# An encoder layer on one core: w_ada loaded as whole rows in two halves of channels behind x, x turned once and kept, rotary angles first, first q and k tiles in pairs

## The chip, the cores and the metric

One Trainium2 chip, of which the kernel uses one core. The time is device time in microseconds (us) of one execution; it is the median over several runs. TensorE is called PE (its weight loads PEld), VectorE DVE, ScalarE ACT, GpSimd POOL, SyncE SP. SP issues nearly all transfers.

## The reference

The layer has one sequence of 512 positions and 1,024 channels. What matters here is its beginning and what first uses it:

```python
mod = silu(c) @ w_ada + b_ada                  # w_ada: 1024 x 3072
shift, scale, gate = split(mod, 3)
h = rms_norm(x, norm_pre) * (1 + scale) + shift
proj = h @ w_in                                # w_in: 1024 x 11264
qa, ka, va, za, qd, kd, vd, zd, gm = split(proj, ...)
qa, ka = rope(qa, positions), rope(ka, positions)
# windowed attention with dilations 1, 4, 16 over qa, ka, va; differential
# attention over qd, kd, vd; gates, two projections, w_out, rms_norm
out = x + gate * rms_norm(y, norm_post)
```

Everything is float32. Before any product with w_in can be made, x's row norms and the first 2,048 columns of `silu(c) @ w_ada` are needed; the gate columns are needed only at the very end.

## The kernel before

**Split products.** A float32 product is made as three passes of rounded operands (`PASSES`): high by high, high by low, low by high. Each operand is cut into `_hi` (an ACT copy in the rounded type) and `_lo` (the difference, made by POOL or DVE).

**Weights.** w_in is cut into blocks of 256 columns, a block into two halves of 4 x 128 channels (k = 0 to 3 and 4 to 7). SP loads a half (512 KB) into one of three `raw` slots (`load_half`, L524), waiting until POOL has made the low part of the half three before. ACT makes the high part (`cut_hi`, L784), POOL the low one (`cut_lo`, L674). Halves 0 to 5 are those of blocks 0 (q), 1 (k) and 2 (v), in the order (0,0), (1,0), (0,1), (1,1), (2,0), (2,1); halves 6, 7 belong to block 3, the next q block.

**Order.** The work is laid out in ticks, and each engine runs through the same ticks in its own program. Tiles 0 to 3, the two q and two k tiles of 128 rows by 512 positions, are computed ahead of tick 8, all four at once, in four PSUM banks of `proj`: for each k the products of all four tiles (L1519 to L1525). Then come four v tiles (ticks 8 to 11), block 3 (ticks 12 to 15) with the first attention step's scores at tick 14, and so on, until PE's last tick.

**The modulation.** For each of the eight k, SP loads two column blocks of w_ada of 128 columns, scale and shift, all 1,024 rows of them (`load_ada`, rows of 512 bytes), into one of two buffers; DVE sums them over the eight row blocks weighted with silu(c) (`sum_ada`, eight instructions of 256 elements per partition); PE sums over the partitions with a matmul against ones (`modulation`, eight small products); three tiny DVE instructions make `ab`, the factor and the offset. PE turns x for that k (`x_turn`, four transposes into `score`), ACT makes `h_f` and `h_hi` from it, POOL `h_lo` (L689), and PE may make the products of that k. Column pair 0 is loaded between x tiles 1 and 2; the others stand in SP's queue among the weights. The buffers are freed by `ada_used`.

**The rotation.** ACT copies a finished q or k tile out of its bank (`rope_copy`, L817); SP's transfers swap the halves of the heads (four issues); DVE multiplies the swapped copy by the sine, POOL the other by the cosine (L704), DVE adds them into `rope_o`, ACT and DVE cut the sum into high and low. For tiles 0 to 3 the copies lie in `zd`, and one swap of four issues (L575) waits for all four copies (`rope_copied` 4). The angles themselves are computed by DVE (L1051 to L1061) after the last `ab`; ACT takes the sines after the four copies (L923, L925). Positions and the rotary constants are loaded by POOL's queue (L652, L653).

**Banks.** Tile 4 + i takes bank i again and waits for the copy of tile i, tile 8 takes the bank of the first v tile and waits until DVE has taken that tile's low part (`bank_free`, L1439). The first scores (`scores`, L1322) wait for the low parts of both q and both k tiles (`rope_lo_done`).

## Time and profile before

| | us |
|---|---|
| three runs: lowest, median, highest | 897.79, 899.67, 900.72 |
| profiled execution: span from first to last instruction (no other time is given with it) | 900.2 |
| PE busy in it | 820.2 (91%) |
| DVE, ACT, POOL busy | 461.5, 360.2, 499.6 |
| first product with w_in starts at | 34.6 |
| first score starts at | 102.5 |

The span is the profiled execution's first to last instruction on this one core. Busy times are sums over an engine's instructions; matmuls are pipelined, and their ends are modelled. "PEclk" or granted clock is the share of 2.4 GHz that was granted to PE: 1.00 is 2.4 GHz, 0.50 is 1.2 GHz. A row of waits says who waited for whom, the total, how often, and the longest.

### The profile page before, as it was taken

To read this page: it belongs to the slowest core of one execution; us is meant where nothing else is said; L and a number is where in the kernel's file an instruction comes from. 1 tells how busy PE (TensorE), PEld (TensorE's weight loads), DVE (VectorE), ACT (ScalarE), POOL (GpSimd) and SP (SyncE) were. 2 spreads that over 40 slices of the span, in tenths; PEclk is the share of its full clock that TensorE was granted. 3 is DMA by queue.
4 is the path that set the end of the run, shared out by engine and by line. 5 is a ranking of instruction groups with operands and counts; after the bars stand their busy time and mean duration, and the time that the engine had idled before them with its cause. 6 is when DMAs were issued, how large, how long until landed. Compare 5 with 4: busy or idle time off the path is not lost.

```text
span 900.2 us, 12651 instructions
## 1 busy us (share of the span) xinstructions
PE 820.2 (91%) x4622; PEld 687.3 (76%) x4622; DVE 461.5 (51%) x743; ACT 360.2 (40%) x774; POOL 499.6 (56%) x657
## 2 busy tenths in 40 slices
PE   1569799999999999999986889999999999999797
PEld 0458579888888888889765668887887778888697
DVE  2885587454444444325466767758756652112122
ACT  3333344344444444333443244545546442313210
POOL 2574555354564656347579665645646456648900
PEclk9999899999999999999999798999999999999899
DMA  9774282223333323223633222222221213324421
GB/s 248 196 213 109 83 277 85 90 76 97 104 107 106 106 84 106 93 95 95 169 110 93 83 67 75 71 82 84 71 71 48 71 48 116 94 71 141 140 90 52
DMA packets 92852, 94.87 MB, mean 105 GB/s; under 512 B 8269, under 2 KB 84086, under 8 KB 92662
## 3 DMA queue, kind: packets, MB, share of 16 engines
q1 hardware_dynamic: 92496, 93.64, 34.2%
q0 software_dynamic: 240, 0.39, 0.5%
q8 instruction: 37, 0.61, 0.3%
q14 instruction: 25, 0.20, 0.1%
q10 hardware_dynamic: 54, 0.02, 0.0%
HBM read 78.21 MB, written 5.34 MB: 93 GB/s over the span
## 4 chain that ended last, share of the span: by engine, by line
PE 60%; POOL 12%; DVE 9%; issue 7%; DMA 5%; ACT 4%; SPq 3%; DVEq 0%; POOLq 0%; ACTq 0%
PE proj L1482 41%; POOL w_lo L679 6%; PE score L1361 4%; PE proj L1565 4%; PE sums L1407 3%; DMA ada<-in_w_ada 3%; PE turned L1378 3%; PE sums L1409 2%; PE score L1336 2%; POOL rope_x L704 1%; DVE ada_sum L1014 1%; POOL h_lo L679 1%; DVE dstat L1128 1%; ACT junk L909 1%; DMA rope_s<-rope_x 1%
## 5 line engine op out<-in xcount | busy, mean ns | idle before, releaser
L679 POOL TENSOR_TENSOR w_lo<-raw,w_hi 128x256 fp32r<-128x256 f32 x408 | 328.2, 836 | 222.2 <-ACT w_hi L793 222.0
L1482 PE MATMUL proj<-h_hi,w_hi 128*128 128x512 f32 x608 | 253.5, 417 | 9.5 <-POOL h_lo L689 8.2
L1482 PE MATMUL proj<-h_hi,w_lo 128*128 128x512 f32 x608 | 241.7, 397 | 0.0
L1482 PE MATMUL proj<-h_lo,w_hi 128*128 128x512 f32 x608 | 240.7, 396 | 0.0
L1482 PEld LDWEIGHTS proj<-h_hi,w_hi 128*128 128x128 f32 x608 | 116.4, 191 | 45.8 <-issue 10.3
L1482 PEld LDWEIGHTS proj<-h_hi,w_lo 128*128 128x128 f32 x608 | 116.3, 191 | 26.5
L1482 PEld LDWEIGHTS proj<-h_lo,w_hi 128*128 128x128 f32 x608 | 116.9, 192 | 21.1
L793 ACT ACTIVATE w_hi<-raw 128x1024 fp32r<-128x1024 f32 x102 | 106.3, 1053 | 13.0 <-PE proj L1482 7.7
L704 POOL TENSOR_TENSOR rope_x<-rope_x,cos_t 128x512 f32<-128x512 f32 x36 | 55.1, 1531 | 86.7 <-DMA rope_s<-rope_x 86.7
L1151 DVE TENSOR_TENSOR at_lo<-turned,at_hi 128x512 fp32r<-128x512 f32 x64 | 44.0, 687 | 64.6 <-ACT at_hi L895 64.0
L877 ACT ACTIVATE probs<-score,dstat 128x512 f32<-128x512 f32 x64 | 43.4, 684 | 59.4 <-DVE dstat L1128 59.4
L1407 PE MATMUL sums<-v,at_hi 128*128 128x128 f32 (+1 forms) x256 | 61.2, 309 | 4.6 <-DVE at_lo L1151 4.6
L885 ACT ACTIVATE probs<-score,rows_out 128x128 f32<-128x128 f32 (+1 forms) x96 | 37.5, 400 | 67.2 <-DVE rows_out L1135 67.2
L1409 PE MATMUL sums<-v,at_lo 128*128 128x64 f32 (+1 forms) x256 | 57.7, 234 | 0.0
L895 ACT ACTIVATE at_hi<-turned 128x512 fp32r<-128x512 f32 x64 | 38.1, 595 | 45.0 <-PE turned L1378 44.5
L1378 PE MATMUL turned<-ident,probs 128*128 128x128 f32 x256 | 39.7, 278 | 17.0 <-DVE za L1226 13.9
L1407 PEld LDWEIGHTS sums<-v,at_hi 128*128 128x128 f32 x256 | 48.5, 190 | 7.9 <-DVE at_lo L1151 6.3
L1378 PEld LDWEIGHTS turned<-ident,probs 128*128 128x128 f32 x256 | 31.1, 142 | 26.8 <-DVE za L1226 15.0
L1409 PEld LDWEIGHTS sums<-v,at_lo 128*128 128x128 f32 x256 | 48.9, 191 | 2.0
L1482 PE MATMUL proj<-w_hi,h_hi 128*128 128x256 f32 x160 | 46.6, 291 | 0.0
L1482 PE MATMUL proj<-w_lo,h_hi 128*128 128x256 f32 x160 | 45.3, 283 | 0.0
L1482 PE MATMUL proj<-w_hi,h_lo 128*128 128x256 f32 x160 | 45.2, 283 | 0.0
(236 smaller groups left out, 1523.0 us busy)
## 6 DMA issues: line engine op xcount, KB each, us to landing
raw<-in_w_in SPq DMA_DIRECT2D x88, 512.0 KB, 3.6
rope_s<-rope_x SPq DMA_DIRECT2D x144, 64.0 KB, 2.3
ada<-in_w_ada SPq DMA_DIRECT2D x16, 512.0 KB, 6.2
zd<-in_w_ada SPq DMA_DIRECT2D x8, 512.0 KB, 5.1
raw<-in_w_proj_b SPq DMA_DIRECT2D x8, 512.0 KB, 3.4
raw<-in_w_out SPq DMA_DIRECT2D x8, 512.0 KB, 3.4
...
```

The lines of the kernel that those rows point to most:

```text
L679: ins = nc.gpsimd.tensor_tensor(lo[:, k, :], raw[:, n % RAW, k, :], hi.bitcast(F32)[:, k, :], ALU.subtract)
L704: nc.gpsimd.tensor_tensor(at, at, cos_t[:], ALU.mult).then_inc(rope_cos_done, 1)
L793: nc.scalar.activation(w_place(half)[0], raw[:, n % RAW, :, :], ACT.Copy).then_inc(w_hi_done, 1)
L877: ins = nc.scalar.activation(probs[:, s.s % 2, i, :], score[:, i, :], ACT.Exp, bias=dstat[:, s.s % 2, i:i + 1], accum_out=den0(s) if i == ...
L885: ins = nc.scalar.activation(probs[:, s.s % 2, 0, i * w:(i + 1) * w], score[:, s.s % 2, i * w:(i + 1) * w], ACT.Exp, bias=rows_out[:, qt, ...
L895: nc.scalar.activation(at_hi[:, s.s % 2, :], turned[:], ACT.Copy).then_inc(t_hi_done, 1)
L1151: tt_(at_lo[:, s.s % 2, :], turned[:], at_hi[:, s.s % 2, :].bitcast(F32), ALU.subtract).then_inc(t_read, 1)
L1361: ins = mm(bank[:, i * w + at:i * w + at + n_k], q[a][rows_, s.head // 2, qt * P:(qt + 1) * P], k[b][rows_, s.head // 2, key:key + n_k], s ...
L1378: ins = nc.tensor.transpose(turned[:, m * P:(m + 1) * P], probs[:, s.s % 2, 0, m * P:(m + 1) * P], ident[:])
L1407: mm(sums[:, to:to + 2 * width].rearrange("p (w e) -> p w e", w=2), hi[:, col:col + P], v[:, kt, :, col0:col0 + width], start=first, stop= ...
L1409: ins = mm(sums[:, to:to + width], lo[:, col:col + P], v[:, kt, 0, col0:col0 + width], start=False, stop=last, skip_group_check=True)
L1482: ins = mm(dst, left, right, start=k == 0 and n == 0, stop=k == nk - 1 and n == 2)
```

## The change

- `ada` holds all eight row blocks of half of the channels: SP loads, behind the four x tiles and raw halves 0 and 1, eight pieces of 512 KB for channels 0 to 511 (rows of 2 KB, scale and shift), then eight for channels 512 to 1,023, each into the place of the piece of the first half, once DVE has used it. Raw halves 2 and 3 stand behind all of them.
- DVE's sums take eight instructions of 1,024 elements per half; `modulation` and `modulate` run twice.
- All eight k of x are turned ahead of the modulation, into six PSUM banks, and ACT copies them to `xt`, which is `zd`'s memory; `h_f` and `h_hi` read `xt`.
- `h_lo` of k = 4 to 7 is made by DVE, of k = 0 to 3 by POOL. The masks are made ahead of the first `cut_lo`.
- PE makes k = 0 to 3 for all four tiles, with the second modulation ahead of k = 3, then k = 4 to 7 for tiles 0 and 1, then for tiles 2 and 3. The swap is made in two pairs, ahead of loads 7 and 8.
- The angles stand first in DVE's queue, ahead of x's mean; the sines follow the scaling of x on ACT. Positions and constants are loaded by ACT's queue.

```diff
         x_in = sb("x_in", [P, NT, D], on=begin)
-        ada = sb("ada", [P, 2, KT, 2, P], on=begin)
-        ada_sum = sb("ada_sum", [P, 2, 2, 2, P], on=begin)
-        h_f = sb("h_f", [P, 2, S], on=begin)
+        ada = sb("ada", [P, KT, 2, S], on=begin)
+        ada_sum = sb("ada_sum", [P, 2, 2, S], on=begin)
...
+        xt = zd
+        def turn_place(k):
+            return score[:, k % 6, :] if k % 6 < 2 else proj[:, k % 6 - 2, :]
...
-            def load_ada(k):
-                if k >= 2:
-                    sp.wait_ge(ada_used, 2 * (k - 1))
-                src = w_ada[0].rearrange("(a p) n -> p a n", p=P)
-                for i in range(2):
-                    sp.dma_start(ada[:, k % 2, :, i, :],
-                                 src[:, :, i * D + k * P:i * D + (k + 1) * P]).then_inc(ada_loaded[k % 2], 16)
+            ada_rows = w_ada[0].rearrange("(a p) (r n) -> p a r n", p=P, r=3)
+            def load_ada(half, kk):
+                if half:
+                    sp.wait_ge(ada_used, kk + 1)
+                sp.dma_start(ada[:, kk, :, :], ada_rows[:, kk, 0:2, half * S:(half + 1) * S]).then_inc(ada_loaded[kk], 16)
...
             for tt in range(NT):
-                if tt == 2:
-                    load_ada(0)
                 sp.dma_start(x_in[:, tt, :], x[0, tt * P:(tt + 1) * P, :]).then_inc(x_loaded[tt], 16)
             load_half(0)
             load_half(1)
-            load_ada(1)
-            load_ada(2)
+            for half in range(2):
+                for kk in range(KT):
+                    load_ada(half, kk)
             load_half(2)
-            load_ada(3)
             load_half(3)
-            for k in range(4, KT):
-                load_ada(k)
...
             for n in range(4, next_half):
+                if n in (7, 8):
+                    pair = n - 7
+                    sp.wait_ge(rope_copied, 2 * pair + 2)
+                    for i in range(4):
+                        j = i ^ 1
+                        sp.dma_start(zd[32 * i:32 * i + 32, 4 + 2 * pair:6 + 2 * pair, :],
+                                     zd[32 * j:32 * j + 32, 2 * pair:2 * pair + 2, :]).then_inc(first_swapped[pair], 16)
                 load_half(n)
...
+            masks()
             for half in prep_at(-1)[:2]:
                 cut_lo(half)
-            for k in range(KT):
+            for k in range(KT // 2):
                 pool.wait_ge(h_hi_done, k + 1)
                 nc.gpsimd.tensor_tensor(h_lo[:, k, :], h_f[:, k % 2, :], h_hi[:, k, :].bitcast(F32),
                                         ALU.subtract).then_inc(h_lo_done, 1)
-                if k in (1, 2, 4, 6):
-                    cut_lo(halves[2 + (1, 2, 4, 6).index(k)])
-                if k == 3:
-                    masks()
+            for half in prep_at(-1)[2:]:
+                cut_lo(half)
             for t in range(8, LAST_TICK + 1):
-                for half in prep_at(t) if t < 12 else []:
-                    cut_lo(half)
-                for tile in tiles[:4] if t == 8 else rope_at(t) if t >= 12 else []:
+                for tile in tiles[2 * (t - 8):2 * (t - 7)] if t < 10 else rope_at(t) if t >= 12 else []:
                     swapped_wait(pool, tile)
                     if rope_no[tile.u] == 0:
                         pool.wait_ge(act_sin, 2)
                     at = rope_place(tile)[0]
                     nc.gpsimd.tensor_tensor(at, at, cos_t[:], ALU.mult).then_inc(rope_cos_done, 1)
-                for half in prep_at(t) if t >= 12 else []:
+                for half in prep_at(t):
                     cut_lo(half)
...
+            act.dma_start(rope_c[:], rope_rows).then_inc(pos_loaded, 16)
+            act.dma_start(merged[:].bitcast(I32), positions[0].partition_broadcast(P)).then_inc(pos_loaded, 16)
...
+            act.wait_ge(angle_done, 1)
+            nc.scalar.activation(sin_t[:], rope_s, ACT.Sin).then_inc(act_sin, 1)
+            act.wait_ge(angle_done, 2)
+            nc.scalar.activation(cos_t[:], rope_o[:], ACT.Sin).then_inc(act_sin, 1)
             for half in prep_at(-1)[:2]:
                 cut_hi(half)
             for k in range(KT):
                 act.wait_ge(x_turned, k + 1)
-                act.wait_ge(ab_done, k + 1)
-                if k >= 2:
+                nc.scalar.activation(xt[:, k, :], turn_place(k), ACT.Copy).then_inc(xt_done, 1)
+            for k in range(KT):
+                act.wait_ge(ab_done, k // 4 + 1)
+                act.wait_ge(xt_done, k + 1)
+                if k >= 6:
+                    act.wait_ge(h_lo_late, k - 5)
+                elif k >= 2:
                     act.wait_ge(h_lo_done, k - 1)
-                nc.scalar.activation(h_f[:, k % 2, :], score[:, k % 2, :], ACT.Identity, bias=ab[:, 1, k:k + 1],
+                nc.scalar.activation(h_f[:, k % 2, :], xt[:, k, :], ACT.Identity, bias=ab[:, 1, k:k + 1],
                                      scale=ab[:, 0, k:k + 1]).then_inc(h_f_done, 1)
-                nc.scalar.activation(h_hi[:, k, :], score[:, k % 2, :], ACT.Identity, bias=ab[:, 1, k:k + 1],
+                nc.scalar.activation(h_hi[:, k, :], xt[:, k, :], ACT.Identity, bias=ab[:, 1, k:k + 1],
                                      scale=ab[:, 0, k:k + 1]).then_inc(h_hi_done, 1)
-                if k in (1, 2, 4, 6):
-                    cut_hi(halves[2 + (1, 2, 4, 6).index(k)])
+                if k >= 3:
+                    for half in prep_at(-1)[k - 1:k] if k < KT - 1 else []:
+                        cut_hi(half)
             act.wait_ge(lam_dots, 1)
             nc.scalar.activation(lam[:, 2:4], lam[:, 0:2], ACT.Exp).then_inc(act_lam, 1)
...
-            act.wait_ge(angle_done, 1)
-            nc.scalar.activation(sin_t[:], rope_s, ACT.Sin).then_inc(act_sin, 1)
-            act.wait_ge(angle_done, 2)
-            nc.scalar.activation(cos_t[:], rope_o[:], ACT.Sin).then_inc(act_sin, 1)
...
-            def sum_ada(k):
-                dve.wait_ge(ada_loaded[k % 2], 32 * (k // 2 + 1))
-                if k >= 2:
-                    dve.wait_ge(mod_done, k - 1)
...
-            sum_ada(0)
...
-            dve.wait_ge(cols_done, 2)
-            for k in range(KT):
-                if 0 < k < KT - 1:
-                    sum_ada(k + 1)
-                mod = (turned, sums)[k % 2]
...
+            def sum_ada(half, kk):
+                dve.wait_ge(ada_loaded[kk], 16 * (half + 1))
+                total = ada_sum[:, half]
+                if kk == 0:
+                    ins = ts_(total, ada[:, kk], silu_c[:, 1, 0:1], None, ALU.mult)
+                else:
+                    dve.wait_ge(ada_used, KT * half + kk)
+                    ins = stt(out=total, in0=ada[:, kk], scalar=silu_c[:, 1, kk:kk + 1], in1=total,
+                              op0=ALU.mult, op1=ALU.add)
+                ins.then_inc(ada_used, 1)
+            def modulate(half):
+                mod, ks = (turned, sums)[half], slice(4 * half, 4 * half + 4)
+                at = lambda first: cols[:, first + 4 * half:first + 4 * half + 4]
+                dve.wait_ge(mod_done, half + 1)
+                link(tt_(ab[:, 0, ks], mod[:, 0:4], at(16), ALU.add))
+                link(stt(out=ab[:, 0, ks], in0=ab[:, 0, ks], scalar=1.0, in1=at(32), op0=ALU.add, op1=ALU.mult))
+                tt_(ab[:, 1, ks], mod[:, 4:8], at(8), ALU.add).then_inc(ab_done, 1)
+            dve.wait_ge(pos_loaded, 32)
...
+            dve.wait_ge(act_x_sq, NT)
+            ts_(st[:, 4:8], st[:, 0:4], 1.0 / D, EPS, ALU.mult, ALU.add).then_inc(x_mean_done, 1)
+            dve.wait_ge(rows_turned, 2)
+            nc.vector.tensor_copy(cols[:, KT:41], sums[:, KT:41]).then_inc(cols_done, 1)
+            dve.wait_ge(pow_done, 1)
+            for tt in range(2):
+                ts_(x_in[:, tt, :], x_in[:, tt, :], st[:, 8 + tt:9 + tt], None, ALU.mult).then_inc(x_norm_done, 1)
+            dve.wait_ge(cols_done, 2)
+            for kk in range(KT):
+                sum_ada(0, kk)
+            modulate(0)
+            for kk in range(KT):
+                sum_ada(1, kk)
+            dve.wait_ge(small_loaded, 64)
...
+            modulate(1)
+            for k in range(KT // 2, KT):
+                dve.wait_ge(h_f_done, k + 1)
+                dve.wait_ge(h_hi_done, k + 1)
+                tt_(h_lo[:, k, :], h_f[:, k % 2, :], h_hi[:, k, :].bitcast(F32), ALU.subtract).then_inc(h_lo_late, 1)
...
-            def modulation(k):
-                if k >= 2:
-                    pe.wait_ge(ab_done, k - 1)
-                if k == 1:
-                    pe.wait_ge(cols_done, 2)
-                pe.wait_ge(ada_used, 2 * (k + 1))
+            def modulation(half):
+                pe.wait_ge(ada_used, KT * (half + 1))
                 for i, side in enumerate((1, 0)):
-                    for part in range(2):
-                        ins = mm((turned, sums)[k % 2][:, i:i + 1], ada_sum[:, k % 2, part, side, :], ones[:, 0:1],
-                                 start=part == 0, stop=part == 1)
+                    for k in range(4):
+                        ins = mm((turned, sums)[half][:, 4 * i + k:4 * i + k + 1], ada_sum[:, half, side, k * P:(k + 1) * P],
+                                 ones[:, 0:1], start=True, stop=True, skip_group_check=True)
                 ins.then_inc(mod_done, 1)
             def x_turn(k):
-                if k == 0:
-                    pe.wait_ge(x_norm_done, 2)
-                    pe.wait_ge(x_norm_act, 2)
-                if k >= 2:
-                    pe.wait_ge(h_hi_done, k - 1)
+                if k >= 6:
+                    pe.wait_ge(xt_done, k - 5)
                 for tt in range(NT):
-                    ins = nc.tensor.transpose(score[:, k % 2, tt * P:(tt + 1) * P], x_in[:, tt, k * P:(k + 1) * P], ident[:])
+                    ins = nc.tensor.transpose(turn_place(k)[:, tt * P:(tt + 1) * P], x_in[:, tt, k * P:(k + 1) * P], ident[:])
                 ins.then_inc(x_turned, 1)
+            pe.wait_ge(x_norm_done, 2)
+            pe.wait_ge(x_norm_act, 2)
+            for k in range(KT):
+                x_turn(k)
+            pe.wait_ge(cols_done, 2)
             modulation(0)
-            x_turn(0)
-            for k in range(KT):
-                if k + 1 < KT:
-                    modulation(k + 1)
-                    x_turn(k + 1)
+            pe.wait_ge(xt_done, KT)
+            for k in range(KT // 2):
+                if k == 3:
+                    modulation(1)
                 pe.wait_ge(h_lo_done, k + 1)
                 for tile in tiles[:4]:
                     products(tile, [k])
+            for pair in (tiles[0:2], tiles[2:4]):
+                for k in range(KT // 2, KT):
+                    pe.wait_ge(h_lo_late, k - 3)
+                    for tile in pair:
+                        products(tile, [k])
...
```

The cut parts of the DVE program are in the section on the kernel: the angles (L1052 to L1061) stay as they are and now stand between `modulate` and the mean of x, and the lambda dots (L1045 to L1049) stand behind the sums of the second half. The single swap of L572 to L575 is gone.

## Rows read from the trace of the kernel before

**Rows 1.** Busy time by stretch: us from:to, length, busy (x instructions), granted clock, DMA share, GB/s.

```profile
34.50:78.90 44.40, 35.73 (x173) 29.17 (x172) 33.01 (x77) 15.81 (x23) 25.87 (x35) 0.92 0.65 184
78.90:90.30 11.40, 11.40 (x96) 11.26 (x94) 6.15 (x12) 4.24 (x6) 6.69 (x7) 1.00 0.55 138
90.30:102.50 12.20, 6.10 (x25) 4.24 (x24) 10.62 (x16) 5.04 (x9) 5.67 (x6) 0.97 0.14 44
102.50:108.70 6.20, 6.17 (x19) 4.87 (x20) 0.69 (x1) 3.92 (x8) 5.53 (x8) 0.51 0.27 87
120.00:390.00 270.00, 270.00 (x1591) 229.84 (x1591) 134.95 (x173) 119.59 (x308) 141.97 (x149) 1.00 0.33 101
390.00:600.00 210.00, 190.12 (x1072) 155.97 (x1071) 127.91 (x207) 85.00 (x178) 135.14 (x176) 0.96 0.33 97
```

**Rows 2.** Waits of PE: 34.4 to 102.5 us, then 102.4 to 390.

```profile
PE proj L1482 <- POOL h_lo L689: 8.2, 4, 3.6
PE proj L1482 <- DVE v L1102: 1.1, 1, 1.1
...
PE score L1350 <- DVE k_lo L1095: 5.0, 1, 5.0
```

**Rows 3.** Busy time of PE's product line (L1482) alone, in two stretches of twelve products.

```profile
34.50:38.70 4.20, 4.07 (x12) 1.00 1.13 319
52.10:55.00 2.90, 2.84 (x12) 1.00 0.52 135
```

**Rows 4.** The chain that ended last, its start: from us, us, what.

```profile
54.93 6.30 DMA raw<-in_w_in
...
81.42 4.94 DMA zd<-zd
```

**Rows 5.** Timeline of the start, ACT, DVE and PE: start us, us, engine, line, what.

```profile
18.86 1.87 PE L1503 MATMUL turned<-ones,ada_sum 128*128 128x1 f32 x8 [13.92 <-DVE ada_sum L1014]
...
19.49 0.17 DVE L1024 TENSOR_SCALAR st<-st 128x4 f32<-128x4 f32 x1 [0.68 <-ACT gate_row L782]
...
20.81 2.19 ACT L797 ACTIVATE x_in<-x_in,st 128x1024 f32<-128x1024 f32 x2 [1.36 <-POOL st L684]
```

**Rows 6.** Transfers: packets and rates from 0 to 9 us, then from 9 to 13.

```profile
DMA packets 2106, 2.14 MB, mean 237 GB/s; under 512 B 118, under 2 KB 1792, under 8 KB 2106
...
DMA packets 441, 0.35 MB, mean 88 GB/s; under 512 B 58, under 2 KB 369, under 8 KB 441
...
q0 software_dynamic: 111, 0.14, 83.1%
```

**Rows 7.** DVE's angle chain, groups of instructions by line: busy us, mean ns.

```profile
L1060 DVE SCALAR_TENSOR_TENSOR rope_x<-rope_x 128x512 f32<-128x512 f32 x1 | 0.7, 683 | 0.0
...
L1058 DVE TENSOR_SCALAR rope_x<-rope_x 128x512 f32<-128x512 f32 x1 | 0.4, 427 | 0.0
```

**Rows 8.** Groups of ACT by line, 20 to 83 us, shapes kept apart, and one of POOL, 24 to 58.

```profile
L808 ACT ACTIVATE h_f<-score,ab 128x512 f32<-128x512 f32 x8 | 6.2, 774 | 28.9 <-DVE ab L1039 15.0 <-issue 13.9
L793 ACT ACTIVATE w_hi<-raw 128x1024 fp32r<-128x1024 f32 x5 | 5.1, 1046 | 0.0
...
L923 ACT ACT_TABLE_LOAD x1 | 1.3, 1283 | 0.0
...
L689 POOL TENSOR_TENSOR h_lo<-h_f,h_hi 128x512 fp32r<-128x512 f32 x5 | 7.0, 1402 | 9.7 <-ACT h_hi L810 9.7
```

**Rows 9.** Transfers from 34 to 42 us, then from 115 to 119.

```profile
DMA packets 4378, 2.47 MB, mean 309 GB/s; under 512 B 70, under 2 KB 4378, under 8 KB 4378
...
DMA packets 456, 1.67 MB, mean 418 GB/s; under 512 B 48, under 2 KB 48, under 8 KB 456
```

**Rows 10.** The gate's sums on DVE (L1256), 128x1024: shortest, median, longest ns.

```profile
L1256 DVE SCALAR_TENSOR_TENSOR gate_row<-zd,silu_c,gate_row x7: 1272/1758/2306, 117.1 to 146.1; 128x1024 f32<-128x1024 f32 x7
```

**Rows 11.** DVE's timeline, the rotation of tiles 2 and 3, first and last instruction.

```profile
96.97 0.68 DVE L1078 TENSOR_TENSOR zd<-zd,sin_t 128x512 f32<-128x512 f32 x1
...
101.78 0.69 DVE L1095 TENSOR_TENSOR k_lo<-rope_o,k_hi 128x512 fp32r<-128x512 f32 x1 [0.36 <-ACT k_hi L831]
```

54 lines of the change are left out of this document (11 added, 43 removed).

## The prediction

> **What bounds the kernel now.** I first read busy time by stretch. From 120 to 390 us PE is busy 270.00 of 270.00 us at full clock; in the 68 us from the first product (34.5) to the first score (102.5) it is busy 53.2 us (35.73 + 11.40 + 6.10) [rows 1]. So the start is where PE lacks work, and what follows runs at PE's pace. PE's waits put names on it: 8.2 us for h_lo, 1.1 us for a bank that DVE had not emptied, 5.0 us for k_lo [rows 2]. Between waits it is slow as well: a k of twelve products takes 2.84 us in a warm stretch, but the first k after the long pause took 4.07 [rows 3], and after the 5 us wait the granted clock is 0.51, that is 1.2 GHz, for 6 us [rows 1]. The chain of waits shows what is behind h_lo and k_lo: a weight half that SP had queued behind the w_ada columns takes 6.30 us to come, and the swap of the heads' halves 4.94 [rows 4]. So the start is a chain "w_ada columns, sum, modulation, h, products" run eight times, then a rotation that waits for all four tiles. A microsecond by which the first score comes earlier should be a microsecond off the end. One stretch speaks against that: from 390 to 600 PE is busy 190.12 of 210.00 [rows 1]. The weights it waits for there are cut behind waits on PE's own products (`cut_hi`), so I take those stalls to move with PE.
>
> **The new order, step by step** (times from the span's start).
>
> *x first.* Before, x's mean stood at 19.49 [rows 5]. In the first 9 us the transfers carried 2.14 MB; from 9 to 13 lies a hole of 88 GB/s, in which POOL's own queue takes 83% of the engines for 0.14 MB [rows 6]. The lambda rows stay on that queue, so I keep the hole. x and the positions are 2.36 MB: in at about 10, the last square at 12. But DVE now does the angles ahead of the mean. Positions (0.26 MB) are issued on ACT's queue at about 2.5, beside the first two x tiles (1.05 MB): 1.31 MB at some 300 GB/s (the 2.14 MB of rows 6 went in the seven us that transfers ran) are in at 7. Bounds: 5.6 at 418 GB/s [rows 9], and 13, the end of the hole. The chain is seven short instructions of 0.43 to 0.48 and five long ones of 0.68 us alone [rows 7]: 6.5 us, ending at 13.5. Mean at 13.7, 5.8 us sooner. From mean to scaling 1.3, scaling 2.19 on ACT [rows 5]: 17.2; DVE's share ends at 16.5.
>
> *ACT.* Table load 1.28, two sines 1.2, two weight halves 2.1, eight new copies of turned x out of PSUM at under 0.77 each (h_f is the nearest row), some 5.3 [rows 8]: 27.1. PE's 32 turns lie beside this. The copies end before the modulation does and so cost nothing; without that cover, 5.3.
>
> *First half of w_ada.* x, raw halves, positions and lambda rows are 3.55 MB; after the hole, at the 309 to 418 GB/s of rows 9, the last raw lands at about 16.2. Then 4.19 MB in 2 KB rows: 309 was reached with rows of 512 bytes and 1 KB, 418 with 4 KB [rows 9]; I take 360, so 11.7 us: 27.9. The second half, piece by piece behind the sums, is in at 39.5. DVE now takes 8 instructions of 1,024 elements for 32 of 256. One takes 1.27 alone, 1.76 in the median and 2.31 at worst beside POOL [rows 10], the first of a half 0.75 as the scaling of x does. POOL writes the masks and cuts halves 0 and 1 meanwhile: 0.75 + 3 x 1.6 + 4 x 2.0 = 13.6, from 16.5: 30.1. Bounds: 29.2 (27.9 + 1.27) and 33.4 (0.75 + 7 x 2.31). Modulation: eight small products 1.87 [rows 5], three tiny DVE instructions 0.6: 32.6. h_f and h_hi 1.5, h_lo 1.4 [rows 8]: first product at 35.5. Before: 34.6. **The start of the products is a loss of 0.9 us.**
>
> *k = 0 to 3.* h comes every 1.5 us from ACT and 1.4 from POOL, PE needs 2.8: no gap. The first k takes 4.0, two more 2.8 each [rows 3]: 45.1.
>
> *Second half.* DVE from 32.6: 0.75 + 7 x 1.8 (POOL has h_lo and half 2 to cut beside it) = 13.4: 46.0. Bounds: 41 (last piece at 39.5) and 49.5. The lambda dots, 1.1, and three tiny instructions: ab at 47.7; PE's part 0.95 is done meanwhile. PE waits 45.1 to 47, makes k = 3 by 49.8, and h_lo of k = 4 is there at 47.7 + 1.5 + 0.7 = 49.9. Now ACT sets the pace, with a weight half of 1.0 between two k: 2.5 us each, k = 7 at 57.4. A k of one pair is 1.4 us of work, so the pair ends at 58.8, and the second pair, with all its inputs there, takes 4 x 1.4: 64.4. Before: 78.9. **14.5 us**, of which the one start above is -0.9 and the seven gaps and slow k after it 15.4. The weights come in time: raw 2 lands at 41.5, its low part is ready by 46, raw 5 follows at 50 and is wanted at 55.
>
> Row and rule can be weighed here. Beside POOL the long DVE instruction grew by 0.49 and 1.04 us [rows 10]. The Trainium skill, SBUF — State Buffer, section Who interferes with whom, makes the port pair that the two engines share an exclusive lock: who comes second blocks until the other instruction is through. By it four sums against an h_lo would take 1.27 + 1.40 each and two against a part of w_lo 1.27 + 0.7, and the second half 0.75 + 4 x 2.67 + 1.27 + 2 x 1.97 = 16.6, an estimate: 3.2 us more than mine, total 880. Rows 10 agree that they block each other, not that it is each time in full.
>
> *v block and first score.* v 11.4 [rows 1]: 75.8. **Bank wait 1.2 gone:** tiles 0 and 1 are copied by 60, swapped by about 65 (4.94 [rows 4]), and their rotation lies under the v block, so DVE takes the first v tile at about 68, 8 us before its bank is wanted. Products of the next q tile 2 x 2.84 = 5.7 (6.0 before): **81.5 for the first score.** Is k_lo there? Tiles 2 and 3 are copied at 65.7, swapped at 71, POOL's cosine product at 73; tiles 2 and 3 took 5.5 us from 96.97 to 102.47 before [rows 11]: 79. Yes, by 2.5 us: **5.0 us gone.** The four more issues of SP cost it 2.4 us each pair with two raw slots full: nothing.
>
> *After the score.* The 6.2 us at a clock of 0.51 [rows 1] held 3.1 us of loss. Half 9 and the pieces of the gate columns behind it come forward less than PE does, so I credit 2.0.
>
> **Sum.** 14.5 + 1.2 + 0.3 + 5.0 = 21.0 to the score, and 2.0: 23.0 us. Span 900.2 - 23.0 = 877.2. The page gives that execution no other time; 900.2 lies between the median 899.67 and the highest 900.72. Forecast: **877**.
>
> **Removed work worth nothing.** 48 of 64 small modulation products leave PE where it waited; four h_lo leave POOL, which waited too. SP's blocked issues behind `ada_used` release no one earlier than rows 9's rates do.
>
> **Rivals.**
> - *The rotation still ends last* (0.14). The last of the four swap issues was out at 81.4 [rows 4], 21.1 us ahead of the score. It would now be out 1.9 after the copies at 65.7; the same distance gives 88.7, 7.2 later: 884. For it: DVE takes v tiles between rotations, POOL's cosine products stand before half 6. Against: two of four tiles are under the v block.
> - *DVE bounds the start* (0.17). All long sums at 2.31 [rows 10]: 33.4 + 2.5 + 16.9 = 52.8 for 46.0: 6.8 later, 884. Positions at 13 instead of 7 give 6 us: 883. It shows as PE idle before k = 3.
> - *DVE hardly meets POOL* (0.08). Sums bound by transfers: k = 4 up to 5 us sooner, 869 to 872.
> - *The early time is given back* (0.04): 390 to 600 is paced by something not tied to PE. Time 900.
> - *Slower* (0.03). The angles stand at the head of DVE's queue; x's mean, the scaling and all sums are queued behind the positions' landing. Each microsecond after 7 is one lost (6 of them up to the end of the hole). From 33 us on the kernel is slower: 23.0 eaten and 2.7 more, 903. For it only the hole of rows 6.
> - *As forecast* (0.54): 873 to 882.
>
> **Range.** 869 to 887: below, the free DVE; above, the 884 of two rivals and 3 us for a clock that falls in the pair phase, where PE works 1.4 of each 2.5 us. Runs lie within 0.3% of each other, so 2.7 us can be told. Faster 0.54 + 0.14 + 0.17 + 0.08 = 0.93; same 0.04; slower 0.03.
>
> **What will show it.** x's mean at 14; eight sums ending near 30 and 46; first product within 2 us of 35.5; second pair without a gap from 59 to 64; first score at 81.5, no wait before it, clock 1.00 after it; PE 270 of 270 in the long stretch. Wrong would be: positions landing late, long sums at 2.3, a score that waits for k_lo, or PE idle later that was not there before.

## The result, and the profile of the changed kernel

The changed kernel took **892.92 us** (median of 4 runs, 892.13 to 893.5), the kernel before, run beside it, 900.19. The ratio is 0.9917 with a 95% interval of 0.9900 to 0.9934. So it is faster by some 7 us, a third of the 23 that were forecast, and 892.92 lies above the range of 869 to 887. The sign was right, the size was not.

The span of the profiled execution is 891.3 us; that of before is 900.2, the forecast for it 877.2. The miss to be explained is 14.1 us. First the stretches (columns: busy time and count for PE, PEld, DVE, ACT and POOL, then PE's granted clock, the DMA share and GB/s), which answer to [rows 1]:

```profile
20.00:40.80 20.80, 9.93 (x49) 9.70 (x50) 15.63 (x16) 13.47 (x20) 17.71 (x23) 0.77 1.03 372
40.80:54.00 13.20, 12.64 (x54) 10.23 (x55) 12.08 (x13) 3.85 (x5) 12.13 (x7) 0.84 0.03 10
54.00:70.40 16.40, 13.97 (x58) 10.23 (x57) 6.04 (x11) 11.28 (x15) 9.73 (x12) 1.00 0.36 98
70.40:89.00 18.60, 17.66 (x124) 16.25 (x123) 16.72 (x18) 7.75 (x13) 13.66 (x12) 1.00 0.48 140
102.00:106.40 4.40, 0.42 (x2) 0.00 (x0) 3.98 (x6) 2.75 (x7) 0.46 (x1) 1.00 1.01 359
106.40:115.00 8.60, 8.58 (x33) 7.12 (x34) 7.35 (x9) 4.29 (x12) 5.83 (x5) 0.60 0.99 326
```

The products of the first four tiles now end at 70.9 (78.7 before, each read from the start of the v block), and the v block with the next q tile keeps PE busy 17.66 of 18.60 us. But a hole stands where none was forecast: from 102.0 to 106.4 PE works 0.42 us, and then it goes at 1.2 GHz, half its upper level (mean granted clock 0.60 up to 115.0). PE's waits from 0 to 130 us, which answer to [rows 2], give it a name (us in total, times, longest):

```profile
PE turned L1505 <- DVE ada_sum L1017: 4.3, 1, 4.3
PE turned L1384 <- DVE at_lo L1157: 4.0, 1, 4.0
PE proj L1488 <- issue: 3.9, 1, 3.9
...
PE proj L1488 <- DVE h_lo L1067: 2.3, 3, 1.2
...
PE score L1356 <- DVE k_lo L1101: 0.9, 1, 0.9
PE sums L1505 <- DVE ada_sum L1017: 0.6, 1, 0.6
```

The waits for h_lo shrank from 8.2 to 2.3 and that for k_lo from 5.0 to 0.9, as the prediction had it. New is the one for `at_lo`, 4.0 us. Now the start itself, DVE's timeline, to be read beside [rows 5]:

```profile
12.36 0.43 DVE L1031 CAST rope_x<-merged 128x512 f32<-128x512 int32 x1 [7.48 <-DMA merged<-in_positions]
...
19.09 0.16 DVE L1043 TENSOR_SCALAR st<-st 128x4 f32<-128x4 f32 x1
...
21.91 0.88 DVE L1014 TENSOR_SCALAR ada_sum<-ada,silu_c 128x1024 f32<-128x1024 f32 x1
22.91 10.18 DVE L1017 SCALAR_TENSOR_TENSOR ada_sum<-ada,silu_c,ada_sum 128x1024 f32<-128x1024 f32 x7
36.82 0.16 DVE L1026 TENSOR_TENSOR ab<-turned,cols 128x4 f32<-128x4 f32 x1 [3.73 <-PE turned L1505]
...
37.29 0.74 DVE L1014 TENSOR_SCALAR ada_sum<-ada,silu_c 128x1024 f32<-128x1024 f32 x1
38.14 13.53 DVE L1017 SCALAR_TENSOR_TENSOR ada_sum<-ada,silu_c,ada_sum 128x1024 f32<-128x1024 f32 x7
...
53.71 0.16 DVE L1026 TENSOR_TENSOR ab<-sums,cols 128x4 f32<-128x4 f32 x1 [0.50 <-PE sums L1505]
```

DVE stands 7.48 us until the positions are there, at 12.36, and the mean of x follows the angles at 19.09, though the last square on ACT was done at 13.9. That is nearly where it stood before (19.49). The sums themselves went well: the first half took 11.2 us (13.6 forecast), the second 14.4 (13.4 forecast). PE's timeline for the same time:

```profile
33.24 3.54 PE L1505 MATMUL turned<-ones,ada_sum 128*128 128x1 f32 x16 [4.26 <-DVE ada_sum L1017]
40.65 0.77 PE L1488 MATMUL proj<-h_hi,w_hi 128*128 128x512 f32 x1 [3.87 <-issue]
41.21 0.63 PE L1488 MATMUL proj<-h_lo,w_hi 128*128 128x512 f32 x1
```

The modulation is 16 records, not 8, and takes 3.54 us; the first product starts at 40.65, 5.1 later than forecast and 6.0 later than before. At the other end of the start, DVE's four rotations (k_lo of tile 3 is what the first score waits for):

```profile
70.60 1.83 DVE L1084 TENSOR_TENSOR zd<-zd,sin_t 128x512 f32<-128x512 f32 x1 [4.33 <-DMA zd<-zd]
72.46 2.27 DVE L1094 TENSOR_TENSOR rope_o<-zd 128x448 f32<-128x448 f32 x2
...
76.53 1.22 DVE L1084 TENSOR_TENSOR zd<-zd,sin_t 128x512 f32<-128x512 f32 x1
...
82.42 1.22 DVE L1084 TENSOR_TENSOR zd<-zd,sin_t 128x512 f32<-128x512 f32 x1
...
86.10 0.69 DVE L1084 TENSOR_TENSOR zd<-zd,sin_t 128x512 f32<-128x512 f32 x1
...
88.22 0.69 DVE L1101 TENSOR_TENSOR k_lo<-rope_o,k_hi 128x512 fp32r<-128x512 f32 x1 [0.36 <-ACT k_hi L841]
```

The first score starts at 88.97 (102.5 before): 13.5 us sooner. The span is shorter by 8.9. What eats the rest lies in the 18 us behind it, here on ACT, POOL, SP's queue, DVE and PE in turn. (The second turns are PE's second group of turned attention probabilities, at 106.42; the third follow at 114.94.)

```profile
88.09 1.99 ACT L794 ACTIVATE w_hi<-raw 128x1024 fp32r<-128x1024 f32 x2
89.21 5.58 POOL L682 TENSOR_TENSOR w_lo<-raw,w_hi 128x256 fp32r<-128x256 f32 x8 [4.96 <-ACT w_hi L794]
92.04 3.14 SPq L536 DMA_DIRECT2D raw<-in_w_in  x2
95.23 2.41 SPq L558 DMA_DIRECT2D rope_s<-rope_x  x4
97.68 2.84 SPq L597 DMA_DIRECT2D zd<-in_w_ada  x4
102.15 0.86 DVE L1259 TENSOR_SCALAR gate_row<-zd,silu_c 128x1024 f32<-128x1024 f32 x1 [10.85 <-DMA zd<-in_w_ada]
102.93 0.68 DVE L1141 TENSOR_REDUCE rows_out<-score 128x2 f32<-128x512 f32 x1
105.67 0.69 DVE L1157 TENSOR_TENSOR at_lo<-turned,at_hi 128x512 fp32r<-128x512 f32 x1 [0.27 <-ACT at_hi L905]
106.42 1.08 PE L1384 MATMUL turned<-ident,probs 128*128 128x128 f32 x4 [4.00 <-DVE at_lo L1157]
114.94 0.60 PE L1384 MATMUL turned<-ident,probs 128*128 128x128 f32 x4
```

ACT cuts halves 8 and 9 only behind its last k_hi, so their low parts on POOL begin at 89.21. SP, which issues in order, can load into those slots from 92.04 on, and issues the swap of the next tile and then the gate columns behind that. DVE has the first gate instruction ahead of the row maxima of the second score, and stands for it 10.85 us. PE's next turns need the at_lo behind it. In the kernel before, the same two places, of the waits of PE and of the timelines of PE and DVE:

```profile
PE turned L1378 <- DVE at_lo L1151: 0.7, 1, 0.7
...
119.44 0.66 PE L1378 MATMUL turned<-ident,probs 128*128 128x128 f32 x4 [0.71 <-DVE at_lo L1151]
124.87 0.60 PE L1378 MATMUL turned<-ident,probs 128*128 128x128 f32 x4
...
115.28 0.75 DVE L1253 TENSOR_SCALAR gate_row<-zd,silu_c 128x1024 f32<-128x1024 f32 x1 [9.19 <-DMA zd<-in_w_ada]
```

The gate instruction comes 13.1 us sooner than there (102.15 for 115.28), nearly the whole 13.5. But PE got over its work between score and turns faster, as forecast: its clock is 1.00 there, where [rows 1] had 0.51 for 6 us. The same work, from the first score to the last product ahead of the second turns, took 15.8 us before (102.53 to 118.34) and 13.1 now (88.97 to 102.03), 2.8 less. That went into the wait, which grew by 3.3, from 0.7 to 4.0. Behind the wait PE goes at 1.2 GHz for 6.8 us, and from the second to the third turns it takes 8.5 us where it took 5.4 (106.42 to 114.94, 119.44 to 124.87): 3.1 more. From the third turns to the mark that the ledger below uses, both kernels take 88.9 us. So 3.3 + 3.1 - 2.8 = 3.6 us is the whole loss between score and mark.

**The ledger of the miss**, each line the measured time less the forecast one:

| point | forecast | measured | late | new here |
|---|---|---|---|---|
| first product | 35.5 | 40.65 | 5.1 | 5.1 |
| second pair's end | 64.4 | 70.9 | 6.5 | 1.4 |
| first score | 81.5 | 88.97 | 7.5 | 1.0 |
| span | 877.2 | 891.3 | 14.1 | 6.6 |

The 6.6 behind the score split at a mark that every kernel here has: the first product of the middle scores with `mask_near`, at 213.8 before and 203.8 now, in a stretch in which PE waits for nothing. From score to mark it was 111.3 us and is 114.9, a loss of 3.6 where a credit of 2.0 had been given; and from the mark to the end 686.4 and 687.5, a loss of 1.1 (5.6 and 1.1 make the 6.6 to rounding). So the start is worth **10.0 us** at the mark. Below, each kernel is measured there too, since what follows the mark varies by some us between executions (680.6 to 687.9 us over the kernels here, whose instructions behind it are the same). PE's mean granted clock behind the mark is 0.99 in the shortest, e12, and 0.98 in all others, so the clock has a part in it; how large, no run shows.

### The profile page after: what moved, and what is told of

The parts are those of the page before. It is cut to its first block, busy times and chain, and to the rows that moved or that the text cites. A ratio compares the mean times of both kernels' runs of the same rounds, so it can differ in the third digit from the quotient of the medians.

```text
span 891.3 us, 12543 instructions
## 1 busy us (share of the span) xinstructions
PE 818.0 (92%) x4590; PEld 685.6 (77%) x4590; DVE 455.3 (51%) x681; ACT 364.9 (41%) x782; POOL 504.2 (57%) x651
## 4 chain that ended last, share of the span: by engine, by line
PE 62%; POOL 12%; DVE 10%; issue 7%; ACT 5%; DMA 3%; SPq 1%; ACTq 0%; DVEq 0%; POOLq 0%
PE proj L1488 43%; POOL w_lo L682 6%; PE score L1367 4%; PE proj L1573 4%; PE sums L1413 3%; PE turned L1384 3%; DVE ada_sum L1017 3%; PE score L1342 2%; PE sums L1415 2%; POOL h_lo L682 1%; POOL rope_x L703 1%; DVE dstat L1134 1%; ACT junk L919 1%; DMA merged<-in_positions 1%; ACT probs L887 1%
## 5 line engine op out<-in xcount | busy, mean ns | idle before, releaser
L682 POOL TENSOR_TENSOR w_lo<-raw,w_hi 128x256 fp32r<-128x256 f32 x408 | 332.9, 847 | 216.6 <-ACT w_hi L794 216.4
```

What stands on the lines that cost most here:

```text
L682: ins = nc.gpsimd.tensor_tensor(lo[:, k, :], raw[:, n % RAW, k, :], hi.bitcast(F32)[:, k, :], ALU.subtract)
```

## The experiments

All are edits of the changed kernel unless another is named, each timed beside the kernel before, whose median was 898.2 to 901.0 in the different sets; so medians are compared by their ratios. "Mark" is the start of the first `mask_near` product. Scores, turns and marks come from one trace of each kernel. What one trace can tell is seen on e6: its instructions are those of the kernel before up to the score, and yet score and mark come 1.3 and 1.4 us sooner. So a mark that differs by up to some 1.4 us (e1, e3, e5, e7, e10, e12, e13) says little by itself.

| run | median | ratio (95%) | first score | second turns | third turns | mark | wait for at_lo |
|---|---|---|---|---|---|---|---|
| kernel before | 900.19 | | 102.5 | 119.4 | 124.9 | 213.8 | 0.7 |
| changed kernel | 892.92 | 0.9917 (0.9900 to 0.9934) | 89.0 | 106.4 | 114.9 | 203.8 | 4.0 |
| e1 lambda rows late | 891.06 | 0.9884 (0.9852 to 0.9917) | 86.8 | 104.4 | 114.0 | 202.9 | 4.1 |
| e2 angles late | 888.97 | 0.9871 (0.9842 to 0.9899) | 89.1 | 105.7 | 111.1 | 201.0 | 0.4 |
| e3 gate sums late | 889.57 | 0.9883 (0.9851 to 0.9915) | 88.8 | 102.2 | 107.6 | 202.8 | 1.7, at 115 |
| e5 no pairs | 891.34 | 0.9917 (0.9891 to 0.9943) | 90.3 | 107.1 | 112.5 | 202.4 | 0.8 |
| e6 gate sums late, before | 900.36 | 1.0001 (0.9980 to 1.0022) | 101.3 | 117.1 | 122.4 | 212.4 | none |
| e7 two sums ahead | 893.76 | 0.9947 (0.9923 to 0.9971) | 89.4 | 106.7 | 115.2 | 204.1 | 2.3 |
| e8 positions first | 888.44 | 0.9883 (0.9853 to 0.9914) | 85.1 | 102.7 | 112.2 | 201.1 | 4.2 |
| e9 halves 8, 9 sooner | 888.98 | 0.9895 (0.9871 to 0.9920) | 90.5 | 107.0 | 112.3 | 201.3 | none |
| e10 PE kept busy | 887.09 | 0.9853 (0.9825 to 0.9881) | 89.7 | 106.7 | 115.2 | 204.1 | 2.0 |
| e11 = e8 + e9 | 884.48 | 0.9827 (0.9798 to 0.9856) | 86.7 | 103.2 | 108.5 | 197.5 | none |
| e12 = e11 + e10 | 883.75 | 0.9824 (0.9795 to 0.9854) | 88.0 | 104.2 | 109.6 | 198.5 | none |
| e13 = e11 + e3 | 885.29 | 0.9832 (0.9804 to 0.9859) | 86.8 | 101.7 | 107.0 | 196.9 | none |

### What holds x's mean at 19.1

**e1**, the lambda rows (POOL's own queue) issued behind the power instead of ahead of the masks:

```
-            for i, v in enumerate((lambda_q1, lambda_k1, lambda_q2, lambda_k2)):
-                pool.dma_start(lam_in[:, i, :], ...).then_inc(small_loaded, 16)
...
             nc.gpsimd.tensor_tensor(st[:, 8:12], st[:, 4:8], half_c[:, 0:4], ALU.pow).then_inc(pow_done, 1)
+            for i, v in enumerate((lambda_q1, lambda_k1, lambda_q2, lambda_k2)):
+                pool.dma_start(lam_in[:, i, :], ...).then_inc(small_loaded, 16)
```

> The changed kernel with the four lambda rows issued by GpSimd after the power and not at the start. Theory A (the software queue's rows hold everything behind them from 9 to 11 us, the positions too): positions land at about 9 instead of 12.3, the last x tile by 11, x's mean at about 16 instead of 19.1, and the end comes 2 to 3 us sooner. Theory B (positions stand behind the x tiles on the same sixteen engines): the hole goes, positions still land at 11 to 12.5, less than 1 us at the end.

The positions landed at 10.0 instead of 12.31, the last square came at 11.5 and the mean at 16.73; the first score came 2.2 us sooner, the mark 1.0.

**e8**, in addition the positions and the rotary rows issued first on ACT's queue, ahead of the small rows:

```
+            act.dma_start(rope_c[:], rope_rows).then_inc(pos_loaded, 16)
+            act.dma_start(merged[:].bitcast(I32), positions[0].partition_broadcast(P)).then_inc(pos_loaded, 16)
             act.dma_start(rows[8:32, :], b_ada.rearrange("a (r p) -> (a r) p", p=P)).then_inc(rows_loaded, 16)
...
-            act.dma_start(rope_c[:], rope_rows).then_inc(pos_loaded, 16)
-            act.dma_start(merged[:].bitcast(I32), positions[0].partition_broadcast(P)).then_inc(pos_loaded, 16)
```

> The changed kernel with the positions and rotary constants issued first on ScalarE's queue and the lambda rows after the power. Theory A (positions at the head of VectorE's queue are what delays the mean): positions land at 5 to 6, angles end at 12, mean at 12.5 instead of 19.1; the sums are then bound by transfers, first score about 5 us sooner, end 4 to 6 us sooner. Theory B (issue order on another queue does not matter, all sixteen engines serve x first): positions at 9 to 10 as with the late lambda rows alone, mean at 16.7.

DVE's timeline of this kernel:

```profile
7.08 0.43 DVE L1031 CAST rope_x<-merged 128x512 f32<-128x512 int32 x1 [2.08 <-DMA merged<-in_positions]
...
13.82 0.16 DVE L1043 TENSOR_SCALAR st<-st 128x4 f32<-128x4 f32 x1
...
16.59 0.73 DVE L1014 TENSOR_SCALAR ada_sum<-ada,silu_c 128x1024 f32<-128x1024 f32 x1
17.45 5.46 DVE L1017 SCALAR_TENSOR_TENSOR ada_sum<-ada,silu_c,ada_sum 128x1024 f32<-128x1024 f32 x4
24.59 4.64 DVE L1017 SCALAR_TENSOR_TENSOR ada_sum<-ada,silu_c,ada_sum 128x1024 f32<-128x1024 f32 x3 [1.68 <-DMA ada<-in_w_ada]
```

This is the timeline that the prediction had: positions at 7, mean at 13.8 (13.7 forecast), sums from 16.6 to 29.2. The first score came at 85.1, 3.9 us sooner, and the second turns 3.7, behind a wait of 4.2 us for at_lo. The mark came only 2.7 us sooner, because the stretch at 1.2 GHz behind that wait lasts 10.2 us here, where it lasted 6.8: from the second to the third turns PE takes 9.5 us for 8.5. The sums now wait 1.68 us for a piece: the transfers have become what bounds them.

**e2**, the angle chain moved behind DVE's last h_lo and the two sines behind the copies of the first four tiles; the positions land when they will:

```
-            dve.wait_ge(pos_loaded, 32)
-            link(nc.vector.tensor_copy(rope_x, merged[:].bitcast(I32)))
-            ... (the angle chain)
             dve.wait_ge(act_x_sq, NT)
...
                 tt_(h_lo[:, k, :], ..., ALU.subtract).then_inc(h_lo_late, 1)
+            (the angle chain)
```

> The changed kernel with the rotary angles back behind the last h_lo on VectorE and the sines behind the four rope copies. Theory A (positions and angles at the head of VectorE's queue delay the mean of x, and that delay goes through to the end): mean at 14.1 instead of 19.1, sums of the first half from 17, first score about 5 us sooner (84), end 4 to 5 us sooner. Theory B (the time to the score is not what sets the end: what follows waits for the gate columns anyway): first score sooner, end within 1 us. Theory C (the angles are then late themselves): score waits for k_lo, no gain or a loss of some us.

The mean stood at 14.66 with nothing ahead of it but the squares. The score came no sooner (PE waited 3.7 us for k_lo, because the angles now delay the rotations), yet the mark came 2.8 us sooner. That is the clock and not the angles: behind the wait for k_lo PE goes at 1.2 GHz from 89.4 to 96.2, while it would have had to wait for at_lo anyway, and behind the second turns it goes at full clock (5.4 us to the third turns). e1, e2 and e8 agree on the mean: it stands where the angles, behind the positions' landing, let it. What that cost is read from e8: 3.9 us at the first score and 2.7 at the mark.

### What gives back time behind the first score

**e3**, the gate sums two ticks later (their first four loads as they were, the last four two ticks later with the sums):

```
-    G_TICK = 14
+    G_TICK, G_ADD = 14, 16
...
-                if G_TICK <= t < G_TICK + KT:
-                    kk = t - G_TICK
+                if G_ADD <= t < G_ADD + KT:
+                    kk = t - G_ADD
```

> The changed kernel in which VectorE adds the gate columns of w_ada two ticks later (16 to 23 instead of 14 to 21), their first four loads staying where they are. Theory A (the 4.0 us wait of TensorE for at_lo at 102 us is VectorE standing at the first gate piece, and the clock at 1.2 GHz that follows costs 3 us more): the wait shrinks to about 1 us, the clock stays at 1.00, the end comes 5 to 6 us sooner. Theory B (the swap of the next q tile's heads, issued behind the same weights, holds VectorE as long): 1 us or less.

```profile
102.17 0.66 PE L1384 MATMUL turned<-ident,probs 128*128 128x128 f32 x4
111.47 0.69 DVE L1084 TENSOR_TENSOR rope_s<-rope_s,sin_t 128x512 f32<-128x512 f32 x1 [4.01 <-DMA rope_s<-rope_x]
115.06 0.66 PE L1384 MATMUL turned<-ident,probs 128*128 128x128 f32 x4 [1.66 <-DVE at_lo L1157]
```

The second score's maxima are no longer queued behind a transfer of gate columns, and the wait ahead of the second turns is gone: they start at 102.17 instead of 106.42. So it was the first gate instruction that PE waited for there. DVE stands 5.61 us for the swap of the next tile, up to 100.8, but that ends in time. The third turns are 7.4 us sooner, for no stretch at 1.2 GHz comes between. Most of this is given back further on: DVE stands 4.01 us for the swap of the tile after that, up to 111.47, PE waits 1.7 us for the at_lo behind it at 115.06, and goes at 1.2 GHz for 6.8 us from 115.9 on. The mark is 1.1 us sooner. So the gate columns are one of two things in the way; the other, one turn later, is a swap, and SP issues both. The same edit in the kernel before, **e6**:

> The kernel before with the same two ticks for the gate columns. There TensorE waited only 0.7 us for at_lo. If the gate piece costs only in the changed kernel (TensorE comes to it earlier, the piece does not): 0 to 1 us sooner. If it is a general cost of that order: 4 us or more, and the gain of the change over its own base stays as it was.

900.36 us beside 899.52, ratio 1.0001 (0.9980 to 1.0022): there it changes nothing at the end, since PE's wait at that place was 0.7 (from score to mark 111.1 us for 111.3). The cost is one of the change, not of the gate's place as such.

**e9**, halves 8 and 9 cut two ticks sooner, which moves their cut on ACT and their low parts on POOL, and with them SP's loads, swap and gate columns:

```
-            prep.setdefault(start_tick[b - 1] + h, []).append((b, h))
+            prep.setdefault(start_tick[b - 1] + h - (2 if b == 4 else 0), []).append((b, h))
```

> The changed kernel with halves 8 and 9 cut two ticks sooner (ticks 10 and 11), ahead of the last two rotations on ScalarE and in GpSimd's gap, so that SP comes sooner to the swap of the next q tile and to the gate columns. Theory A (that chain, last rotation, cut of halves 8 and 9, swap, gate columns, at_lo, sets the end): swap issued at about 90.5 instead of 95.2, gate pieces landed by 98, wait for at_lo under 1 us, clock 1.00, end 5 to 7 us sooner. Theory B (the wait moves to another transfer): 1 to 2 us.

```profile
92.19 2.42 SPq L558 DMA_DIRECT2D rope_s<-rope_x  x4
94.65 2.03 SPq L597 DMA_DIRECT2D zd<-in_w_ada  x4
```

SP's swap is out 3.0 us sooner and the first gate instruction runs at 98.60 instead of 102.15. The at_lo that PE had waited for starts at 103.46 instead of 105.67, and the wait is gone. It has a price: POOL's low parts now run beside the rotations, k_lo comes later, and the first score waits 2.7 us and stands at 90.5. The mark is 2.6 us sooner all the same, but not because PE comes sooner to the second turns: it comes there at 106.96, 0.5 later, since it goes at 1.2 GHz from 91.4 to 98.2, behind the wait for k_lo. The gain is what follows: no wait and no stretch at 1.2 GHz behind it, 5.4 us to the third turns instead of 8.5. So this run shows two things at once, a chain through ACT, POOL and SP that is 2.2 us sooner, and a stretch at 1.2 GHz that falls ahead of the turns and not behind them; e5 below has the second without the first.

**e11**, e8 and e9 together. If both only opened the same wait, they would not add.

> The changed kernel with two edits at once: the positions and rotary rows first in ScalarE's queue and the lambda rows behind the power (alone: first product of the middle scores at 201.1 instead of 203.8, time 888.4), and halves 8 and 9 cut two ticks sooner (alone: 201.3, 889.0). Theory chain (each takes away another part of what stands ahead of the maxima of the first score: the one the start of the whole chain, the other the swap of tile 8 and the gate columns): they add, with the middle scores at 198 to 199.5 and the time at 885 to 887.5. Rival same slack (both only open the same wait, the 4.0 us ahead of the first turned probabilities, and the second finds nothing left): 200.5 to 201.5 and 887.5 to 889.

They add, and more: 2.7 + 2.6 = 5.3 expected at the mark, 6.4 measured (197.5), and 884.48 us, a ratio of 0.9827 for 0.9917. The surplus is in the clock again. Beside e9, positions first bring 3.8 us at the first score, at both turns and at the mark alike: the loss that e8 alone had behind its wait does not occur, for there is no such wait. The mark is now 16.3 us ahead of the kernel before.

**e13**, e11 with the gate sums of e3:

> Positions first, lambda rows late, halves 8 and 9 two ticks sooner, and the sums of the gate columns at ticks 16 to 23 instead of 14 to 21. Theory chain: with halves 8 and 9 sooner the gate columns (98.6) no longer stand in the way of the maxima, so putting them later adds nothing: middle scores within 0.7 us of the kernel without this edit. Rival gate: the gate columns, still ahead of the maxima in VectorE's order, cost another 1 to 2 us, and the time falls to 884 to 886.

The second turns are 1.5 us sooner, the mark 0.5 (196.9), the time is 885.29: within what two executions differ by. With halves 8 and 9 sooner, no gain from moving the gate sums is left at the end.

### The pairs and the sums

**e5**, the pairs undone: all four tiles k by k to the end, as in the kernel before.

```
-            for pair in (tiles[0:2], tiles[2:4]):
-                for k in range(KT // 2, KT):
-                    pe.wait_ge(h_lo_late, k - 3)
-                    for tile in pair:
-                        products(tile, [k])
+            for k in range(KT // 2, KT):
+                pe.wait_ge(h_lo_late, k - 3)
+                for tile in tiles[:4]:
+                    products(tile, [k])
```

> The changed kernel with k = 4 to 7 made for all four tiles together, as before; the two swaps stay. Theory A (the serial rotation of four tiles on VectorE, 18 us from the first swap's landing to the last k_lo, sets half 9's cut and with it all that follows): copies of tiles 0 and 1 come some 5 us later, the score waits 5 us for k_lo, the end is 4 to 5 us later. Theory B (the gate columns' landing has slack of its own): first score later, end within 1 us.

The v block starts at 68.14 instead of 70.89: with pairs PE has 1.4 us of work for every 2.4 in which ACT makes a k, and then the second pair still to do, so they end the four tiles 2.8 us later. The swaps go out at 67.6 and 70.8 (66.3 and 71.7 with pairs), and the score comes 1.3 us later after a wait of 3.7 for k_lo. At_lo is no sooner (106.31 for 105.67), and the mark is 1.4 us sooner, since the stretch at 1.2 GHz falls from 90.1 to 97.0, ahead of the second turns and not behind them. The pairs do take most of the wait for k_lo, and no gain of theirs is seen at the end.

**e7**, two sums of the second half put ahead of the first modulation's three tiny instructions, so that DVE works while PE does the modulation:

```
             for kk in range(KT):
                 sum_ada(0, kk)
+            for kk in range(2):
+                sum_ada(1, kk)
             modulate(0)
-            for kk in range(KT):
+            for kk in range(2, KT):
                 sum_ada(1, kk)
```

> The changed kernel with the first two sums of the second half made by VectorE ahead of the first modulation, in the 3.7 us in which it waits for the 16 small products. Theory A (sums of the second half are what holds k = 4 to 7): sums end 2 us sooner (49.5 instead of 51.7), the pair and all after it too, end 2 us sooner. Theory B (TensorE's own products of k = 0 to 3, at half clock for their first 4 us, set the pace): first modulation 0 to 0.5 later, nothing at the end.

The sums of the second half end 2.4 us sooner, but the h_lo of k = 4 comes no sooner (56.40, 55.92 without the edit), and the mark stays (204.1). PE has k = 0 to 2 ahead of the second modulation in its own order; it begins them at 41.57, 0.9 later than without the edit, and is through with them at 52.3. Without the edit it waited 0.56 us for the sums at that place. So past the first product DVE's sums bounded the start by some 0.6 us; the rest is the late first product.

### The clock at the start

**e10**, 52 products of 128x128 by 128x128 whose result nobody uses, in PE's gap ahead of the first modulation:

```
+            def fill(n):
+                for _ in range(n):
+                    mm(sums[:, 256:384], ident_b[:], ident_b[:], start=True, stop=True, skip_group_check=True)
+            fill(16)
+            for kk in (5, 6, 7):
+                pe.wait_ge(ada_used, kk)
+                fill(12)
             modulation(0)
```

> The changed kernel with 52 extra products of 128x128 by 128x128 (bf16, their result is used by nothing) on TensorE in the gap between the last turn of x (29) and the first modulation (33.2): 16 right behind the turns, 12 each behind the fifth, sixth and seventh sum of the first half. Theory clock (the stretch of 13.7 us at 1.2 GHz from 32.3 on comes from TensorE's gap before it, and costs what it slows): the stretch is gone, the first modulation takes some 2.0 us instead of 3.5, the products of k=0 0.4 us each instead of 0.63, and the first score starts 1 to 3 us sooner than 89.0; time 890 to 892. Rival work-bound (the stretch below full clock hides behind VectorE's sums and the low parts of h, which set the pace): the stretch goes but the first score moves by under 1 us, and the time stays at 892 to 893. Rival no cause: the stretch stays as it is.

The granted clock falls to 1.2 GHz at 33.2 for 10.2 us instead of at 31.4 for 13.7, but the modulation still takes 3.06 us (3.54) and the products from 40.01 on still 0.63 each:

```profile
30.92 0.84 PE L1524 MATMUL sums<-ident_b 128*128 128x128 bf16 x12 [0.62 <-DVE ada_sum L1017]
32.58 3.06 PE L1505 MATMUL turned<-ones,ada_sum 128*128 128x1 f32 x16 [0.82 <-DVE ada_sum L1017]
40.01 0.77 PE L1488 MATMUL proj<-h_hi,w_hi 128*128 128x512 f32 x1 [4.36 <-issue]
40.57 0.63 PE L1488 MATMUL proj<-h_lo,w_hi 128*128 128x512 f32 x1
```

The wait between modulation and first product (4.36 us, for ab, h and h_lo) is still there, and the edit does not touch it. Score and mark do not move (89.7 and 204.1 for 89.0 and 203.8). The median is 887.09, a ratio of 0.9853 for 0.9917, clear of the noise, and this I can't put down to the edit: in the traces the gain lies behind the mark (684.1 for 687.5), where the two kernels have the same instructions. The traced execution was the slowest of the six (890.0), so what made the others faster still is in no trace. **e12**, the same with e11:

> The run before this one in the list with the 52 extra products in TensorE's gap ahead of the first modulation as well (their result is used by nothing). Theory clock: 1 to 3 us sooner than without them at the first score and at the middle scores, time 884 to 886. Rival work-bound: under 1 us.

The mark is 198.5 against 197.5 without it, the time 883.75 against 884.48, with intervals that lie over each other. So the extra products bring nothing at the start, and the 887.09 of e10 is not repeated by its own edit in e12.

## Why the prediction was wrong, point by point

**What failed first is the step "Positions ... are in at 7", and with it "Mean at 13.7, 5.8 us sooner".** It shared 300 GB/s between the positions and the first two x tiles as if each got its part. They were there at 12.36, close to the upper bound of 13; the mean stood at 19.09. e8 shows the cause from the other side: issued first, and with POOL's lambda rows out of the way, the positions are there at 7.08 and the mean at 13.82. The mechanism was in the text, as the rival "Slower", with its price of "each microsecond after 7 is one lost" and a chance of 0.03. It did not make the kernel slower, but 5.4 us of its loss came in, which e8 prices at 3.9 at the first score and 2.7 at the mark. The mistake was to take the low end of a bound from 5.6 to 13 for a transfer on which all of DVE's queue hung.

**"Eight small products 1.87".** The row of [rows 5] has 8 records for the modulation of one k, for which the code before issues 4 products of f32, not the eight that the section on the kernel names: each is two records. The change issues 8 products for each half, and so 16 records, as the trace has it. They took 3.54 us at 1.2 GHz, 1.7 more than forecast. I had read records as products; the code stood beside the row. (It also lowers the "removed work": 32 of 64 records, not 48, with no price at either number.)

**"0.75 + 3 x 1.6 + 4 x 2.0 = 13.6".** 11.2 measured; a sum beside POOL's masks took 1.30, the last two beside `w_lo` 1.57. It gave 2.4 back. Together: 5.4 + 1.7 - 2.4, and 0.4 in small steps, are the 5.1 at the first product. "A loss of 0.9" was 6.0.

**Second half, "0.75 + 7 x 1.8".** 14.4 measured for 13.4. The four sums beside POOL's h_lo took about 2.1 us each, and those h_lo 2.06 us on average (8.23 for four) against 1.40 in [rows 8]. By the rule of the Trainium skill, SBUF — State Buffer, section Who interferes with whom, that the second of the two engines blocks until the other is through, I had worked out 16.6, an estimate; the trace lies between the two, nearer to mine, and agrees with the page that each holds the other up, not that every meeting costs the full length of the other's instruction. e7 then showed that these sums held up the h_lo of k = 4 by 0.6 us at most.

**ACT sets the pace, 2.5 us for each k of 4 to 7.** Right: 2.36 us (h_lo at 55.92, 58.28, 60.64, 63.00). The products behind them: the pairs end at 65.4 and 70.9, 5.5 us apart for "4 x 1.4". What was not asked is whether pairs are right under that pace; e5 has the four tiles done 2.8 us sooner without them.

**"Tiles 2 and 3 took 5.5 us ... 79", no wait for k_lo, 5.0 gone.** Wrong in its reasoning, small in its price. With the pairs 6.5 late, k_lo should have been there at 85.5 by that sum; it came at 88.9, and since the v block was late too, the wait was 0.9. The rotations go through DVE one behind the other: tiles 0 and 1 from 70.60 to 82.4, 11.8 us for two beside POOL's work and v tiles, and 2 and 3 behind them, 6.5. From the first landing to the last k_lo it is 18.3 us. I had priced the last two alone and taken the first two as done under the v block.

**"Half 9 and the pieces of the gate columns behind it come forward less than PE does, so I credit 2.0" is the second step that failed, and the larger one at the mark.** The sentence names the mechanism and then gives it the wrong sign. That those come forward less than PE is a wait of PE, not a smaller gain. It came out as 3.6 us lost up to the mark, so 5.6 off. (The clock's own part was right: 2.8 of the 3.1 us came back there, and went into the wait for at_lo; the 1.2 GHz then fell behind that wait instead, and cost 3.1 again.) The wait of 0.7 for at_lo in the kernel before, 17 us behind the score, was the row to look at: PE now comes to that place 16.3 us sooner, the at_lo only 13.0. e3 shows that the gate instruction was what PE waited for there: without it ahead, the second turns start 4.25 us sooner. e9 and e11 show that an earlier cut of halves 8 and 9 makes the chain 2.2 us sooner and leaves no wait; that their whole gain is this chain is not shown, for in both the stretch at 1.2 GHz falls ahead of the turns as well.

**PE's pace from there on.** Right: no wait from 130 to 390 us, and mark to end is 687.5 for 686.4. The 1.1 are not explained; no run was made for it, and the kernels differ by 7.3 in that figure.

**The rivals.** "The rotation still ends last" held in order, with 0.9 us. "DVE bounds the start" was the nearest in effect, though through the positions and not through long sums; it had 883 for that, and was near up to the score (6.5 late at the second pair's end for its 6). No rival stood for a new wait behind the score, and with the two together the range was passed.
